# Where 48 VectorE dot products stand in a one-core transformer kernel: eight instead of twelve in each feed-forward loop, and eight in the output projection between them

## The chip, the cores and the metric

The kernel runs on one NeuronCore of one Trainium2 chip. The engines are named as in the profile: PE is TensorE (PEld its weight loads), DVE is VectorE, ACT is ScalarE, POOL is GpSimd and SP is SyncE. The metric is the device time of one execution in microseconds (us). Three executions of the kernel before took 1374.60, 1374.96 and 1375.77 us; the median is 1374.96 us.

## The reference

Three blocks in float32 are applied to x of 256 tokens by 1024 features: a sparse attention layer with a feed-forward, a retention layer with a feed-forward, and a state-space block whose norms are scaled and shifted by a modulation vector. Only the parts around the change are shown.

```python
def first_block(x, ...):
    for i in range(2):
        h = rms_norm(x, norm_mix_g[i])
        x = x + (dsa_mixer(h, ...) if i == 0 else retention_mixer(h, ...))
        x = x + conv_ffn(rms_norm(x, norm_ffn_g[i]), ...)
    return x

def conv_ffn(h, w_up, conv_w, conv_b, w_down):          # 1024 -> 2 * 2816 -> 1024
    u = h @ w_up
    u = sum(up[:, j:j + seq] * conv_w[j] for j in range(3)) + conv_b
    a, b = u[..., :2816], u[..., 2816:]
    return (jax.nn.silu(a) * b) @ w_down

def retention_mixer(h, w_in, out_g, w_out):
    ...                                                 # four heads
    return y.astype(h.dtype) @ w_out                    # 2048 -> 1024

def second_block(x, c, w_ada, b_ada, ...):
    mod = (jax.nn.silu(c) @ w_ada + b_ada)              # 6 * 1024 values
    shift_m, scale_m, gate_m, shift_f, scale_f, gate_f = jnp.split(mod, 6, axis=-1)
    h = rmsnorm(x, norm_mix_w) * (1.0 + scale_m) + shift_m
    ...
```

The change moves parts of the work on `silu(c) @ w_ada`. It needs nothing of x, and its result is first used after the second feed-forward.

## The kernel before

**Layout and split.** Activations are kept transposed, 128 features on the partitions by 256 tokens. Every float32 product is made of three matmuls: an operand is split into a high part (`w_hi`, `a_hi`, `b_hi`), which ACT makes by a copy, and a low part (`w_lo`, `a_lo`, `b_lo`), which DVE makes by a subtraction, and PE adds high by high, high by low and low by high (`mm3`, lines 182 to 184).

**The weight stream.** Weights come as 381 slabs of 128 by 1024 (512 KB) in the order of their use, through a ring of six buffers. SP loads slab s once DVE has split slab s - 6. `split_hi` on ACT (line 169) and `split_lo` on DVE (line 174) run three slabs ahead of PE. Each slab feeds 24 matmuls of 256 columns. At its end PE counts up `w_used`, for which those who read its result wait.

**The feed-forward** (`ffn_pe`, `ffn_act`, `ffn_vec`) goes over 22 pairs p of 128 columns of `a` and of `b`, three slabs a pair: two up slabs and one down slab. PE does the two up slabs of pair p + 1, and then the down slab of pair p, which needs `b_lo` of pair p (line 822). On DVE a pair is: split a slab, move the first half out of PSUM (`evict`, line 794), split a slab, two convolution taps (800, 802) on what ACT has scaled (741), move out the second half, two more taps, the product (818), split a slab, and `b_lo` (822). DVE and ACT run pairs 0 and 1 in straight code, pairs 2 to 17 in a loop of four turns with four pairs each (`UNROLL`, places u = 0 to 3), and pairs 18 to 21 again in straight code. After the last `b_lo`, `add_down` adds the result to `res` (853).

**The retention** (`retention_pe`, `_act`, `_vec`) is a loop of four turns, one a head with 12 slabs. Then comes the output projection (`out_pe`, `out_act`, `out_vec`) in straight code: eight output tiles m of two slabs. For each m DVE splits two slabs, waits until PE has done the tile, adds it to `res` (310) and makes `a_lo` of the tile before (275). ACT splits two slabs, waits for that add, and makes `a_hi` and the square `sq` of the new tile (266, 271). Both are queues in order, so a tile's slabs on ACT stand behind the add of the tile before on DVE. The second feed-forward's first slab needs `a_lo` and `sq` of all eight tiles, one after the other, and the sum of the squares (PE, 213) is what `vec_inv` (258 to 261) and `spread_inv` (228) turn into the norm's factor.

**The modulation** is 48 tiles of `w_ada` (128 by 1024, 512 KB each). Column i of `mod` is one tile multiplied by the row `silu(c)` and summed, in one DVE instruction (`dot`, line 336) with a short read of its accumulator behind it. POOL loads the tiles (`ada_loads`, line 331) into three buffers taken in turn: the load of tile i waits until dot i - 3 is done. The dots stand at three of the four places of each turn of both feed-forward loops (`LOOP_DOTS_AT = (0, 1, 3)`, 12 dots a loop) and at six places in each head (24 in all). In the loops a dot writes to `head_dots`, and at a turn's end one copy brings its columns to `mod` (837).

Of the kernel before, what the change touches and what calls it, by code (L numbers as in the profile page):

```python
# [21 lines left out]
HEADS_B = 4  # L22
# [13 lines left out]
S_BOUT = S_B + 12 * HEADS_B  # L36
# [10 lines left out]
ADA_TILES = 6 * NT  # L47
# [20 lines left out]
def val(base, it=None, step=0):  # L68

    return base if it is None else it * step + base  # L70
# [21 lines left out]
def build(nc, x, stream, ada, c_rows, params, consts, out):  # L92
    ctx = ExitStack()
    with ctx:
        def sb(name, shape, dt=F32):
            return ctx.enter_context(nc.sbuf_tensor(name, shape, dt))

        def sem(name):
            return ctx.enter_context(nc.semaphore(name))
# [17 lines left out]
        mod = sb("mod", [P, 48])  # L117
# [20 lines left out]
        def pcol(name, at=0, rows=P, n=1):  # L138
            return par[0:rows, COL[name] + at:COL[name] + at + n]
# [142 lines left out]
        def lo_ahead(dve, s, it=None, ds=0):  # L282
            if s < SLABS:
                split_lo(dve, s, it, ds)
# [17 lines left out]
                    hi_ahead(act, s + 3)  # L302
                act_prep(act, v, m, g)

        def out_vec(dve, s0, per, v, g):
            for m in range(NT):
                for s in range(s0 + per * m, s0 + per * (m + 1)):
                    lo_ahead(dve, s + 3)
                dve.wait_ge(w_used, s0 + per * (m + 1))
                dve.tensor_tensor(res[:, m], res[:, m], ps[:, 4 + (m + 2) % 4, 0:SEQ], ALU.add).then_inc(res_ready, 1)  # L310
                if m:
                    vec_prep(dve, v, m - 1, g)
            vec_prep(dve, v, NT - 1, g)


        FFN_DOTS, HEAD_DOTS = 12, 6
        assert 2 * FFN_DOTS + HEAD_DOTS * HEADS_B == ADA_TILES
        ada_base = ARENA - 4 * DM - 8
        top[0] = ada_base
        ada_raw, cond_row, head_dots = area(3, DM), area(DM), area(8)  # L320
        cond_in, cond_ready, mod_ready = sem("cond_in"), sem("cond_ready"), sem("mod_ready")
        ada_landed, dot_done = [sem(f"ada_landed{i}") for i in range(3)], sem("dot_done")

        def ada_loads(pool):

            pool.wait_ge(o_lo_ready, HEADS_A)
            pool.dma_start(cond_row, c_rows).then_inc(cond_in, 16)
            for i in range(ADA_TILES):
                if i >= 3:
                    pool.wait_ge(dot_done, i - 2)  # L330
                pool.dma_start(ada_raw[:, i % 3], ada[i]).then_inc(ada_landed[i % 3], 16)

        def dot(dve, i, o, it=None, per=0):

            dve.wait_ge(ada_landed[i % 3], val(16 * (i // 3 + 1), it, 16 * per // 3))
            dve.tensor_tensor_reduce(ada_raw[:, i % 3], ada_raw[:, i % 3], cond_row, 1.0, 0.0,  # L336
                                     ALU.mult, ALU.add, o).then_inc(dot_done, 1)


# [350 lines left out]

        UNROLL = 4
        LATER = (FF_PAIRS - 4) // UNROLL
        LOOP_DOTS_AT = (0, 1, 3)
        LOOP_DOTS = len(LOOP_DOTS_AT)
        assert LOOP_DOTS * LATER == FFN_DOTS
        assert (FF_PAIRS - 2) % UNROLL == 0
# [88 lines left out]
        def ffn_vec(dve, step, L, s0, v, next_gain):  # L785
            f = ffn_sems[L]

            def prm(p, j, it):
                c = COL[f"ffn{L}"] + 8 * p + j
                return par[:, c:c + 1] if it is None else par[:, bass.ds(it * 8 * UNROLL + c, 1)]  # L790

            def evict(p, half, s, it, ds):
                dve.wait_ge(w_used, val(s + half + 1, it, ds))
                dve.tensor_tensor(up[:, p % 2, half], ps[:, 6 - 2 * (p % 2) + half, 0:SEQ], inv[:, :], ALU.mult).then_inc(f["up_out"], 1)  # L794

            def taps(p, half, it):
                dve.wait_ge(f["tap"], val(2 * p + half + 1, it, 2 * UNROLL))
                t = conv[:, p % 2, half]
                u = up[:, p % 2, half]
                step(dve.scalar_tensor_tensor(out=t[:, 1:SEQ], in0=u[:, 0:SEQ - 1], scalar=prm(p, 3 * half + 1, it),  # L800
                                              in1=t[:, 1:SEQ], op0=ALU.mult, op1=ALU.add))
                dve.scalar_tensor_tensor(out=t[:, 2:SEQ], in0=u[:, 0:SEQ - 2], scalar=prm(p, 3 * half, it),  # L802
                                         in1=t[:, 2:SEQ], op0=ALU.mult, op1=ALU.add).then_inc(f["conv"], 1)

            def pair(p, s, it=None):
                ds = 0 if it is None else 3 * UNROLL
                lo_ahead(dve, s + 3, it, ds)
                if p == 0:
                    vec_inv(dve, step, v, EPS_A)
                    dve.wait_ge(inv_ready, v + 1)  # L810
                evict(p, 0, s, it, ds)
                lo_ahead(dve, s + 4, it, ds)
                taps(p, 0, it)
                evict(p, 1, s, it, ds)
                taps(p, 1, it)
                dve.wait_ge(f["conv"], val(2 * p + 2, it, 2 * UNROLL))
                dve.wait_ge(f["gate"], val(p + 1, it, UNROLL))
                dve.tensor_tensor(glu[:, p % 2], gate[:, p % 2], conv[:, p % 2, 1], ALU.mult).then_inc(f["glu"], 1)  # L818
                if p:
                    lo_ahead(dve, s + 5, it, ds)  # L820
                dve.wait_ge(f["hi"], val(p + 1, it, UNROLL))
                dve.tensor_tensor(b_lo[:, p % 2], glu[:, p % 2], b_hi[:, p % 2].bitcast(F32), ALU.subtract).then_inc(f["operand"], 1)  # L822

            pair(0, s0)
            pair(1, s0 + 2)
            dot0 = L * (FFN_DOTS + HEAD_DOTS * HEADS_B)
            if L == 0:
                dve.wait_ge(cond_ready, 1)
            with dve.Fori(0, LATER) as it:
                step.enter(it, 2 * UNROLL + 1)  # L830
                for u in range(UNROLL):
                    pair(2 + u, s0 + 5 + 3 * u, it)
                    if u in LOOP_DOTS_AT:
                        n = LOOP_DOTS_AT.index(u)
                        dot(dve, dot0 + n, head_dots[:, n:n + 1], it, LOOP_DOTS)
                dve.wait_ge(dot_done, val(dot0 + LOOP_DOTS, it, LOOP_DOTS))
                step(dve.tensor_copy(mod[:, bass.ds(it * LOOP_DOTS + dot0, LOOP_DOTS)], head_dots[:, 0:LOOP_DOTS]))
            step.leave(LATER)
            if L == 1:
                dve.tensor_tensor(mod[:, :], mod[:, :], pcol("b_ada", n=ADA_TILES), ALU.add).then_inc(mod_ready, 1)  # L840
            for p in range(2 + UNROLL * LATER, FF_PAIRS):
                pair(p, s0 + 3 * p - 1)
            lo_ahead(dve, s0 + 3 * FF_PAIRS - 1 + 3)
            add_down(dve, s0 + 3 * FF_PAIRS, v + 1, next_gain)
# [139 lines left out]
        def retention_vec(dve, step):  # L984
# [5 lines left out]
            with dve.Fori(0, HEADS_B) as it:  # L990
# [11 lines left out]
                for j in range(12):  # L1002
                    s = S_B + j
                    split_lo(dve, s + 3, it, HEAD)
                    if j in DOT_AT:
                        n = DOT_AT.index(j)
                        dot(dve, FFN_DOTS + n, head_dots[:, n:n + 1], it, HEAD_DOTS)
                    if j == 1:
                        rotary(q_rot, 0, s + 1)
                    if j == 3:  # L1010
                        dve.wait_ge(rot_ready, val(1, it, 2))
                        rotary(k_rot, 2, s + 1)
                    if j == 7:
                        dve.wait_ge(qk_ready, val(1, it, 1))
                        dve.tensor_tensor(decayed, ps[:, 7, 0:SEEN], con[:, bass.ds(it * SEEN + CC["decay"], SEEN)],
                                          ALU.mult).then_inc(decayed_ready, 1)
                    if j == 10:
                        dve.wait_ge(ret_sum, val(1, it, 1))
                        dve.tensor_scalar(rs_var[:, 0:NB], ps[:, 7, 400:402], 1.0 / 512, EPS_A, ALU.mult, ALU.add).then_inc(var_ready, 1)
                        rsqrt(dve, step, RS_RET, NB, rs_root[:, 0:NB], it)  # L1020
                        step(dve.tensor_scalar(diag[:, 2], ident, rs_root[:, 0:1], None, ALU.mult))
                        dve.tensor_scalar(diag[:, 3], ident, rs_root[:, 1:2], None, ALU.mult).then_inc(ret_diag, 1)
                    if j >= 8:
                        dve.wait_ge(w_used, val(s + 1, it, HEAD))
                        dve.tensor_tensor(g_b[:, j - 8], ps[:, j - 8, 0:SEQ], inv[:, :], ALU.mult).then_inc(g_taken, 1)
# [20 lines left out]
                y_lo(3)  # L1046
                dve.wait_ge(y_operand, val(4, it, 4))
            step.leave(HEADS_B)
            out_vec(dve, S_BOUT, 2, 3, "ffn_g1")


        top[0] = ARENA - 4 * SEQ
# [897 lines left out]
```

## Time and profile before

| | |
|---|---|
| median of the runs | 1374.96 us (1374.60 to 1375.77) |
| the profiled execution | 1374.81 us, of it 1372.8 us from the first to the last instruction |
| mean granted TensorE clock | 0.961 |
| PE, weight loads, DVE, ACT busy | 1277.5, 1238.6, 958.8, 706.3 us |
| first feed-forward's loop on DVE | 174 to 321 us, its pairs end at 351 us |
| retention heads, output projection | 367 to 540 us, 540 to 581 us |
| second feed-forward's loop on DVE | 607 to 753 us, its pairs end at 783 us |

Times in the rows are counted from the first instruction. In an answer in order of time each row is: start, duration, engine, line, operation, what it writes and reads, and in brackets how long the engine was idle before it and what ended that. Durations of instructions that follow each other overlap a little, so a step is read from start to start. A matmul's end is modelled; its start is not.

### The profile page before, as it was taken

To read this page: it belongs to the slowest core of one execution; us is meant where nothing else is said; L and a number is where in the kernel's file an instruction comes from. 1 tells how busy PE (TensorE), PEld (TensorE's weight loads), DVE (VectorE), ACT (ScalarE), POOL (GpSimd) and SP (SyncE) were. 2 spreads that over 40 slices of the span, in tenths; PEclk is the share of its full clock that TensorE was granted. 3 is DMA by queue.
4 is the path that set the end of the run, shared out by engine and by line. 5 is a ranking of instruction groups with operands and counts; after the bars stand their busy time and mean duration, and the time that the engine had idled before them with its cause. 6 is when DMAs were issued, how large, how long until landed. Compare 5 with 4: busy or idle time off the path is not lost.

```text
span 1372.8 us, 27337 instructions
## 1 busy us (share of the span) xinstructions
PE 1277.5 (93%) x9944; PEld 1238.6 (90%) x9944; DVE 958.8 (70%) x1728; ACT 706.3 (51%) x1098; POOL 28.8 (2%) x58
## 2 busy tenths in 40 slices
PE   6877999999899999999999989999999998999997
PEld 6867999999799899999999879898899997999996
DVE  4475688888678877568888868878777555555554
ACT  4334655555545455545555556666666334544442
POOL 0000000000000000000000000000000000000000
PEclk9889999999899999999999979999999998899998
DMA  6321456666366555636665506344345553455540
GB/s 257 123 62 63 175 206 212 218 220 208 108 245 245 189 207 215 211 128 214 229 214 168 199 33 229 132 160 156 135 138 170 183 184 123 139 184 183 183 153 31
DMA packets 70999, 234.54 MB, mean 171 GB/s; under 512 B 7056, under 2 KB 15376, under 8 KB 70304
## 3 DMA queue, kind: packets, MB, share of 16 engines
q1 hardware_dynamic: 63280, 203.87, 43.3%
q0 software_dynamic: 7664, 29.92, 6.3%
q8 instruction: 36, 0.59, 0.2%
q14 instruction: 19, 0.16, 0.0%
HBM read 232.69 MB, written 1.08 MB: 170 GB/s over the span
## 4 chain that ended last, share of the span: by engine, by line
PE 50%; DVE 29%; issue 10%; ACT 8%; DVEq 1%; DMA 0%; ACTq 0%; SPq 0%; PEldq 0%
PE ps L182 15%; PE ps L183 14%; PE ps L184 14%; DVE w_lo L174 11%; DVE arena L800 3%; ACT w_hi L169 3%; DVE arena L794 2%; DVE arena L802 2%; PE ps L213 2%; ACT arena L741 2%; DVE arena L1480 1%; DVE b_lo L822 1%; DVE arena L336 1%; ACT arena L544 1%; PE ps L1220 1%
## 5 line engine op out<-in xcount | busy, mean ns | idle before, releaser
L182 PE MATMUL ps<-a_hi,w_hi 128*128 128x256 f32 x1912 | 560.4, 293 | 11.1 <-DVE a_lo L1080 5.2
L174 DVE TENSOR_TENSOR w_lo<-w_raw,w_hi 128x1024 fp32r<-128x1024 f32 x381 | 462.2, 1220 | 148.6 <-ACT w_hi L169 144.7
L183 PE MATMUL ps<-a_lo,w_hi 128*128 128x256 f32 x1912 | 548.7, 287 | 0.0
L184 PE MATMUL ps<-a_hi,w_lo 128*128 128x256 f32 x1912 | 548.1, 287 | 0.0
L169 ACT ACTIVATE w_hi<-w_raw 128x1024 fp32r<-128x1024 f32 x381 | 387.0, 1046 | 18.8 <-PE ps L184 12.3
L182 PEld LDWEIGHTS ps<-a_hi,w_hi 128*128 128x128 f32 x1912 | 374.3, 196 | 23.2 <-issue 16.5
L183 PEld LDWEIGHTS ps<-a_lo,w_hi 128*128 128x128 f32 x1912 | 375.1, 196 | 0.5 <-issue 0.2
L184 PEld LDWEIGHTS ps<-a_hi,w_lo 128*128 128x128 f32 x1912 | 374.6, 196 | 0.0
L182 PE MATMUL ps<-b_hi,w_hi 128*128 128x256 f32 x928 | 267.1, 288 | 18.0 <-DVE b_lo L822 12.0
L183 PE MATMUL ps<-b_lo,w_hi 128*128 128x256 f32 x928 | 263.3, 284 | 0.0
L184 PE MATMUL ps<-b_hi,w_lo 128*128 128x256 f32 x928 | 263.2, 284 | 0.0
L182 PEld LDWEIGHTS ps<-b_hi,w_hi 128*128 128x128 f32 x928 | 178.5, 192 | 23.8 <-DVE w_lo L174 11.9
L183 PEld LDWEIGHTS ps<-b_lo,w_hi 128*128 128x128 f32 x928 | 178.8, 193 | 0.0
L184 PEld LDWEIGHTS ps<-b_hi,w_lo 128*128 128x128 f32 x928 | 178.7, 193 | 0.0
L741 ACT ACTIVATE arena<-arena,par 128x256 f32<-128x256 f32 x88 | 53.0, 602 | 107.9 <-DVE arena L794 107.9
L800 DVE SCALAR_TENSOR_TENSOR arena<-arena,par 128x255 f32<-128x255 f32 x88 | 42.3, 481 | 37.6 <-ACT arena L741 37.6
L336 DVE CUSTOM_DVE_ANT_0 arena<-arena 128x1024 f32<-128x1024 f32 x48 | 58.5, 1218 | 0.0
L752 ACT ACTIVATE b_hi<-arena 128x256 fp32r<-128x256 f32 x44 | 18.4, 419 | 63.1 <-DVE arena L818 63.1
L1637 ACT ACTIVATE arena<-ps 128x256 f32<-128x256 f32 x32 | 12.3, 384 | 73.6 <-PE ps L184 73.6
L802 DVE SCALAR_TENSOR_TENSOR arena<-arena,par 128x254 f32<-128x254 f32 x88 | 42.5, 483 | 10.2 <-DVE arena L800 2.0
L213 PEld LDWEIGHTS ps<-con,sq 128*128 128x128 f32 x224 | 36.3, 244 | 11.4 <-ACT sq L271 6.3
L213 PE MATMUL ps<-con,sq 128*128 128x1 f32 x224 | 35.6, 279 | 10.2 <-ACT sq L271 5.6
(245 smaller groups left out, 1208.4 us busy)
## 6 DMA issues: line engine op xcount, KB each, us to landing
w_raw<-stream SPq DMA_DIRECT2D x381, 512.0 KB, 3.7
arena<-ada POOLq DMA_DIRECT2D x48, 512.0 KB, 4.7
c_hi<-cum_rows POOLq DMA_DIRECT2D x4, 1024.0 KB, 5.0
con<-consts SPq DMA_DIRECT2D x1, 1440.0 KB, 13.0
arena<-x SPq DMA_DIRECT2D x1, 1024.0 KB, 5.1
out<-arena SPq DMA_DIRECT2D x2, 512.0 KB, 3.4
arena<-c_rows POOLq DMA_DIRECT2D x1, 512.0 KB, 7.7
par<-params SPq DMA_DIRECT2D x1, 319.0 KB, 5.5
```

The lines of the kernel that those rows point to most:

```text
L169: act.activation(w_hi[:, s % RING], w_raw[:, s % RING], ACT.Copy).then_inc(w_hi_ready, 1)
L174: dve.tensor_tensor(w_lo[:, s % RING], w_raw[:, s % RING], w_hi[:, s % RING].bitcast(F32), ALU.subtract).then_inc(w_lo_ready, 1)
L182: pe.matmul(o, wh, xh, start=start, stop=False, skip_group_check=shared)
L183: pe.matmul(o, wh, xl, start=False, stop=False, skip_group_check=shared)
L184: return pe.matmul(o, wl, xh, start=False, stop=stop, skip_group_check=shared)
L213: mm = pe.matmul(ps[:, sum_bank(v), b:b + 1], sq[:, k, b * P:(b + 1) * P], ones[:, 0:1], start=(k == 0 and b == 0), stop=(k == NT - 1), sk ...
L336: dve.tensor_tensor_reduce(ada_raw[:, i % 3], ada_raw[:, i % 3], cond_row, 1.0, 0.0, ALU.mult, ALU.add, o).then_inc(dot_done, 1)
L741: act.activation(conv[:, p % 2, half], up[:, p % 2, half], ACT.Identity, bias=prm(p, 6 + half, it), scale=prm(p, 3 * half + 2, it)).then_i ...
L752: act.activation(b_hi[:, p % 2], glu[:, p % 2], ACT.Copy).then_inc(f["hi"], 1)
L794: dve.tensor_tensor(up[:, p % 2, half], ps[:, 6 - 2 * (p % 2) + half, 0:SEQ], inv[:, :], ALU.mult).then_inc(f["up_out"], 1)
L800: step(dve.scalar_tensor_tensor(out=t[:, 1:SEQ], in0=u[:, 0:SEQ - 1], scalar=prm(p, 3 * half + 1, it), in1=t[:, 1:SEQ], op0=ALU.mult, op1= ...
L802: dve.scalar_tensor_tensor(out=t[:, 2:SEQ], in0=u[:, 0:SEQ - 2], scalar=prm(p, 3 * half, it), in1=t[:, 2:SEQ], op0=ALU.mult, op1=ALU.add). ...
```

## The change

The first loop and the second get two dots a turn instead of three (`LOOP_DOTS_AT = (0, 2)`, eight a loop), the heads keep six each, and the output projection gets eight, one for each tile m, between its slab splits and its wait for PE. These eight write straight to `mod`, with no copy. The buffer of a tile is now from a table: two buffers in turn in the feed-forward loops, three in turn in the heads and the projection. A load waits for the last dot on its buffer.

```diff
-        def out_vec(dve, s0, per, v, g):
+        def out_vec(dve, s0, per, v, g, first_dot):
             for m in range(NT):
                 for s in range(s0 + per * m, s0 + per * (m + 1)):
                     lo_ahead(dve, s + 3)
+                dot(dve, first_dot + m, mod[:, first_dot + m:first_dot + m + 1])
                 dve.wait_ge(w_used, s0 + per * (m + 1))
...
-        FFN_DOTS, HEAD_DOTS = 12, 6
-        assert 2 * FFN_DOTS + HEAD_DOTS * HEADS_B == ADA_TILES
+        FFN_DOTS, HEAD_DOTS, OUT_B_DOTS = 8, 6, 8
+        assert 2 * FFN_DOTS + HEAD_DOTS * HEADS_B + OUT_B_DOTS == ADA_TILES
+        DOT_BUF = [n % 2 for n in range(FFN_DOTS)] + [n % 3 for n in range(HEAD_DOTS * HEADS_B + OUT_B_DOTS)] + [n % 2 for n in range(FFN_DOTS)]
+        DOT_LOAD = [DOT_BUF[:i + 1].count(DOT_BUF[i]) for i in range(ADA_TILES)]
+        DOT_LAST = [max([j for j in range(i) if DOT_BUF[j] == DOT_BUF[i]], default=-1) for i in range(ADA_TILES)]
...
-                if i >= 3:
-                    pool.wait_ge(dot_done, i - 2)
-                pool.dma_start(ada_raw[:, i % 3], ada[i]).then_inc(ada_landed[i % 3], 16)
+                if DOT_LAST[i] >= 0:
+                    pool.wait_ge(dot_done, DOT_LAST[i] + 1)
+                pool.dma_start(ada_raw[:, DOT_BUF[i]], ada[i]).then_inc(ada_landed[DOT_BUF[i]], 16)
...
-        LOOP_DOTS_AT = (0, 1, 3)
+        LOOP_DOTS_AT = (0, 2)
...
-            out_vec(dve, S_BOUT, 2, 3, "ffn_g1")
+            out_vec(dve, S_BOUT, 2, 3, "ffn_g1", FFN_DOTS + HEAD_DOTS * HEADS_B)
```

DVE at the end of a turn of the feed-forward loop, before: `b_lo` of the last pair (822), the dot (336, two rows), the copy to `mod` and the next turn.

```order
L822 TENSOR_TENSOR b_lo<-arena,b_hi 128x256 [waits ffn0_hi]
L336 ISA arena<-arena 128x1024 [waits ada_landed2]
L336 ISA arena 128x1
L836 ISA
L837 ISA [waits dot_done]
L837 COPY mod<-arena 128x3
L82 REGISTER_ALU
```

The same place in the changed kernel:

```order
L826 TENSOR_TENSOR b_lo<-arena,b_hi 128x256 [waits ffn0_hi]
L840 ISA
L841 ISA [waits dot_done]
L841 COPY mod<-arena 128x2
L82 REGISTER_ALU
```

The turn's last pair has lost its dot; the one that stood in the second pair now stands in the third.

DVE at the start of the output projection, before: two splits (174), the add to `res` (310) that waits for PE, and from the second tile on `a_lo` (275).

```order
L990 COMPARE_AND_BRANCH
L174 TENSOR_TENSOR w_lo<-w_raw,w_hi 128x1024 [waits w_hi_ready] x2
L310 TENSOR_TENSOR res<-res,ps 128x256 [waits w_used]
L174 TENSOR_TENSOR w_lo<-w_raw,w_hi 128x1024 [waits w_hi_ready] x2
L310 TENSOR_TENSOR res<-res,ps 128x256 [waits w_used]
L275 SCALAR_TENSOR_TENSOR a_lo<-res,par,a_hi 128x256 [waits a_hi_ready]
```

The same place in the changed kernel, where the dot is line 340:

```order
L994 COMPARE_AND_BRANCH
L174 TENSOR_TENSOR w_lo<-w_raw,w_hi 128x1024 [waits w_hi_ready] x2
L340 ISA arena,mod<-arena 128x1024 [waits ada_landed0]
L340 ISA mod 128x1
L311 TENSOR_TENSOR res<-res,ps 128x256 [waits w_used]
L174 TENSOR_TENSOR w_lo<-w_raw,w_hi 128x1024 [waits w_hi_ready] x2
L340 ISA arena,mod<-arena 128x1024 [waits ada_landed1]
L340 ISA mod 128x1
L311 TENSOR_TENSOR res<-res,ps 128x256 [waits w_used]
L275 SCALAR_TENSOR_TENSOR a_lo<-res,par,a_hi 128x256 [waits a_hi_ready]
```

Each of the eight adds now stands behind a dot, and with it ACT's work on the tile.

## Rows read from the trace of the kernel before

**Rows 1.** The page, busy time of each engine and its share of the span.

```profile
PE 1277.5 (93%) x9944; PEld 1238.6 (90%) x9944; DVE 958.8 (70%) x1728; ACT 706.3 (51%) x1098; POOL 28.8 (2%) x58
```

**Rows 2.** Waits of PE in 175 to 351 and in 600 to 783: total, times, longest.

```profile
PE ps L182 <- DVE b_lo L822: 4.3, 11, 0.8
...
PE ps L182 <- DVE b_lo L822: 5.7, 10, 2.1
```

**Rows 3.** Waits of DVE, the longest in 315 to 352 and in 606 to 783.

```profile
DVE arena L800 <- ACT arena L741: 3.6, 5, 0.9
...
DVE arena L800 <- ACT arena L741: 17.4, 20, 0.9
```

**Rows 4.** Instructions in order of time, DVE, one turn of the first feed-forward's loop.

```profile
192.01 0.42 DVE L822 TENSOR_TENSOR b_lo<-arena,b_hi 128x256 fp32r<-128x256 f32 x1
192.35 1.22 DVE L336 CUSTOM_DVE_ANT_0 arena<-arena 128x1024 f32<-128x1024 f32 x1
...
193.49 1.22 DVE L174 TENSOR_TENSOR w_lo<-w_raw,w_hi 128x1024 fp32r<-128x1024 f32 x1
...
201.17 0.42 DVE L822 TENSOR_TENSOR b_lo<-arena,b_hi 128x256 fp32r<-128x256 f32 x1
...
209.23 0.42 DVE L822 TENSOR_TENSOR b_lo<-arena,b_hi 128x256 fp32r<-128x256 f32 x1
...
211.68 1.23 DVE L174 TENSOR_TENSOR w_lo<-w_raw,w_hi 128x1024 fp32r<-128x1024 f32 x1 [0.58 <-DVE mod L837]
...
219.45 0.42 DVE L822 TENSOR_TENSOR b_lo<-arena,b_hi 128x256 fp32r<-128x256 f32 x1
```

**Rows 5.** The same, PE: first matmuls of three down slabs in the last pairs.

```profile
337.43 0.28 PE L182 MATMUL ps<-b_hi,w_hi 128*128 128x256 f32 x1
...
346.07 0.28 PE L182 MATMUL ps<-b_hi,w_hi 128*128 128x256 f32 x1
...
351.15 0.39 PE L182 MATMUL ps<-b_hi,w_hi 128*128 128x256 f32 x1 [2.04 <-DVE b_lo L822]
```

**Rows 6.** The same, DVE: last pair of the first feed-forward.

```profile
347.07 0.42 DVE L794 TENSOR_TENSOR arena<-ps,inv 128x256 f32<-128x256 f32 x1
...
350.68 0.42 DVE L822 TENSOR_TENSOR b_lo<-arena,b_hi 128x256 fp32r<-128x256 f32 x1
```

**Rows 7.** The same, DVE: output projection, and start of the second feed-forward.

```profile
544.58 0.41 DVE L310 TENSOR_TENSOR res<-res,ps 128x256 f32<-128x256 f32 x1
546.83 2.36 DVE L174 TENSOR_TENSOR w_lo<-w_raw,w_hi 128x1024 fp32r<-128x1024 f32 x2 [1.83 <-ACT w_hi L169]
549.11 0.42 DVE L310 TENSOR_TENSOR res<-res,ps 128x256 f32<-128x256 f32 x1
...
581.41 0.42 DVE L310 TENSOR_TENSOR res<-res,ps 128x256 f32<-128x256 f32 x1 [1.15 <-PE ps L184]
...
582.41 0.48 DVE L275 SCALAR_TENSOR_TENSOR a_lo<-res,par,a_hi 128x256 fp32r<-128x256 f32 x1 [0.18 <-ACT a_hi L266]
583.66 1.23 DVE L174 TENSOR_TENSOR w_lo<-w_raw,w_hi 128x1024 fp32r<-128x1024 f32 x1 [0.77 <-ACT w_hi L169]
587.37 0.16 DVE L258 TENSOR_SCALAR rs_var<-ps 128x2 f32<-128x2 f32 x1 [2.49 <-PE ps L213]
...
588.91 0.29 DVE L261 TENSOR_SCALAR diag<-con,inv_tok 128x128 f32<-128x128 f32 x1
```

**Rows 8.** The same, PE: sum of the last tile's squares, and the norm's spread.

```profile
586.83 0.50 PE L213 MATMUL ps<-con,sq 128*128 128x1 f32 x4
...
590.51 0.59 PE L228 MATMUL ps<-diag,con 128*128 128x256 f32 x2
```

**Rows 9.** Stretches: busy time of PE, PEld, DVE, ACT, POOL; clock; DMA share, GB/s.

```profile
381.00:395.00 14.00, 14.00 (x77) 12.12 (x76) 10.26 (x16) 3.85 (x6) 1.59 (x3) 1.00 0.90 322
...
540.00:586.00 46.00, 45.84 (x384) 45.63 (x383) 26.85 (x34) 23.97 (x35) 0.00 (x0) 1.00 0.56 184
```

**Rows 10.** Line 331, all 48 loads of modulation tiles: issue to landing.

```profile
DMA to landing us min/median/max: 3.8/4.7/10.0
```

More of the change, by code:

```diff
@@ L328, in ada_loads, with dot @@
             for i in range(ADA_TILES):
-                if i >= 3:
-                    pool.wait_ge(dot_done, i - 2)
-                pool.dma_start(ada_raw[:, i % 3], ada[i]).then_inc(ada_landed[i % 3], 16)
-        def dot(dve, i, o, it=None, per=0):
-            dve.wait_ge(ada_landed[i % 3], val(16 * (i // 3 + 1), it, 16 * per // 3))
-            dve.tensor_tensor_reduce(ada_raw[:, i % 3], ada_raw[:, i % 3], cond_row, 1.0, 0.0,
+                if DOT_LAST[i] >= 0:
+                    pool.wait_ge(dot_done, DOT_LAST[i] + 1)
+                pool.dma_start(ada_raw[:, DOT_BUF[i]], ada[i]).then_inc(ada_landed[DOT_BUF[i]], 16)
+        def dot(dve, i, o, it=None, loads=0):
+            dve.wait_ge(ada_landed[DOT_BUF[i]], val(16 * DOT_LOAD[i], it, 16 * loads))
+            dve.tensor_tensor_reduce(ada_raw[:, DOT_BUF[i]], ada_raw[:, DOT_BUF[i]], cond_row, 1.0, 0.0,
                                      ALU.mult, ALU.add, o).then_inc(dot_done, 1)
@@ L825, in ffn_vec @@
             pair(1, s0 + 2)
-            dot0 = L * (FFN_DOTS + HEAD_DOTS * HEADS_B)
+            dot0 = L * (ADA_TILES - FFN_DOTS)
             if L == 0:
@@ L834, in ffn_vec @@
                         n = LOOP_DOTS_AT.index(u)
-                        dot(dve, dot0 + n, head_dots[:, n:n + 1], it, LOOP_DOTS)
+                        dot(dve, dot0 + n, head_dots[:, n:n + 1], it, LOOP_DOTS // 2)
                 dve.wait_ge(dot_done, val(dot0 + LOOP_DOTS, it, LOOP_DOTS))
@@ L1006, in retention_vec @@
                         n = DOT_AT.index(j)
-                        dot(dve, FFN_DOTS + n, head_dots[:, n:n + 1], it, HEAD_DOTS)
+                        dot(dve, FFN_DOTS + n, head_dots[:, n:n + 1], it, HEAD_DOTS // 3)
                     if j == 1:
```

## The prediction

> **What bounds the kernel now.** I first read the engines' shares [rows 1]: PE is busy for 93% of the span, DVE for 70%. By that alone, DVE instructions would cost nothing wherever they stand. So I read next who waits for whom in the feed-forwards, where the change takes dots away. PE waits there for `b_lo` of line 822, 11 times in the first and 10 times in the second [rows 2]. DVE waits for ACT and for itself, and its two lists hold no wait for PE, not even in the last pairs, where no dot stands [rows 3]. That is the point on which all rests: DVE is the slower engine for the whole of both feed-forwards. It enters the loop about level with PE, falls behind, and is still catching up when the last pair ends.
>
> The sizes come from one turn of the loop [rows 4]. From one `b_lo` to the next is 9.16 us where a dot stands between (192.01 to 201.17), 8.06 where none does (201.17 to 209.23), and 10.22 with the turn's last dot, the copy and the branch (209.23 to 219.45). Four pairs are 9.16 + 9.16 + 8.06 + 10.2 = 36.6 us. PE needs 8.64 us for a pair's 72 matmuls when nothing holds it (337.43 to 346.07) [rows 5], so 34.56 a turn: DVE is 2.0 us a turn behind. In the straight code after the loop its pair is about 7.5 us and it catches up, but in the last pair `evict` starts at 347.07 [rows 6], one microsecond after PE had the operand's slab done (346.07) [rows 5], and PE then stands 2.04 us before its last down slab, until `b_lo` of 350.68 is there. So the feed-forward ends with DVE's last `b_lo`, and everything behind it follows in a chain.
>
> The output projection is the opposite. From 564 us on DVE waits 1.15 us in each tile for PE (581.41 is the last) [rows 7], and weight loads are busy for 45.63 of 46 us [rows 9]. PE needs 2 x 2.88 = 5.76 us a tile (2.88 is a third of 8.64).
>
> **The change part by part.**
>
> *Four dots fewer in each feed-forward.* A dot takes DVE from 192.35 to 193.49, 1.14 us, with the accumulator's read inside it [rows 4]. Between pairs it shows as 9.16 - 8.06 = 1.10, because without it DVE waits 0.04 for ACT's split; at the turn's end there is no such wait. The new turn is 9.16 + 8.06 + 9.16 + (10.2 - 1.15) = 35.43 us, 1.15 less. Since DVE is never held by PE, the last `b_lo` comes 4 x 1.15 = 4.6 us earlier, and nothing else is late in its place until PE's own floor. That floor has to be worked out. A turn now keeps PE waiting for 35.43 - 34.56 = 0.87 us where it was 2.04. Before, PE lost 7.0 us on the way to its slab of 346.07; after, three turns and the first dot of the fourth make 3 x 0.87 + 0.5 = 3.1, so that slab starts 3.9 to 4.0 earlier, at 342.1. The last pair's `evict` comes 4.6 earlier, at 342.5. DVE is still the later of the two by 0.3 us, so the 4.6 is got in full, and there is hardly any more to be got. The second feed-forward is the same code; it starts 1.1 us better (ACT does the `silu` of c only in the first), the same steps give the same margin, and again 4.6. Sum: 9.2 us.
>
> Bounds for the turn's end, which the trace does not show without a dot: the copy waits for the dot's semaphore, and about 0.2 us a turn may go with it; but the register work for the copy and the branch, which ran under the dot, may now come out by as much. So 1.15 +- 0.2 a turn, 3.8 to 5.4 a loop. I take the middle, since the two are alike in size.
>
> *Eight dots in the output projection.* By count there is room: 1.15 us of waiting a tile, and a dot is 1.14. But the tile is a round through two queues, and the first tiles have to be read, where DVE is behind and nothing waits for PE. From one add to the next are 4.53 us (544.58 to 549.11) [rows 7]: add, ACT's `a_hi` and `sq`, ACT's first split, DVE's two splits. The dot stands in this round, not beside it, so the round becomes 4.53 + 1.15 = 5.68 us, 0.08 less than PE's 5.76. DVE starts the projection late, and now never catches up: the first add comes at 544.58 + 1.15 = 545.73, the eighth at 545.73 + 7 x 5.68 = 585.49, where it was 581.41 [rows 7]. That is 4.1 us later. PE is not held inside the projection: the split for its sixth slab ends at 549.2 (545.73 + 2.25 + 1.2), and PE, whose last slab ends at 581.2, comes to that slab at 549.5; from there the room grows by 0.08 a tile.
>
> What does the late last add hold? `a_lo` of the last tile begins 1.0 after the add and takes 0.48, so it is there at 587.0; PE took that tile at 586.83 [rows 8], because it had to do seven others first. So PE loses 0.2 to 0.3 us here, not 4.1. DVE's next split moves with ACT from 583.66 to 587.7 and ends at 588.9, so `vec_inv` starts at 588.9 instead of 587.37, 1.5 later, and its last step ends at 588.91 + 0.29 + 1.5 = 590.7 [rows 7]. PE comes to the spread at 590.51 + 0.3 [rows 8]. They meet within 0.1. Everything from there to the first down slab is one chain, so I charge 0.35 us. Ends: 0, if DVE's operations overlap better; 2.5, if the round is 5.9 instead of 5.68, when the last add comes 1.5 later still, `vec_inv` with it, and PE stands 0.3 longer.
>
> *Two buffers in the feed-forwards.* A load waits for the dot two before and has more than 17 us (two pairs) to land, and the 48 loads took 3.8 to 10.0 [rows 10]. In the projection a tile is asked for three rounds ahead, 15 us. Both cost nothing. The added traffic is 8 x 0.52 MB in 46 us, 91 GB/s on top of 184 [rows 9]. That is 275, and 322 was moved in the stretch from 381 us [rows 9].
>
> *The heads* keep their dots and their places. Nothing is charged.
>
> Sum against the profiled execution: 1374.81 - 9.2 + 0.35 = 1365.96. That execution lies 0.15 below the median, so I say **1366.0 us**.
>
> **The rivals.**
>
> *1. The turn's end gives a little more.* 0.2 us a turn saved at the copy gives 2 x 5.3 = 10.6, which is also PE's floor, since the evict would then start as PE ends. With a projection that costs nothing this is 1374.81 - 10.6 = 1364.2, and runs of one kernel spread over 1.2 us, so 1363.0 to 1364.6. For it: the wait for the dot's semaphore is real. Against it: the register rows stay.
>
> *2. Only part comes through.* If PE, not DVE, sets the last pairs, only the shorter waits for `b_lo` are won, 3.9 a loop: 1374.81 - 7.8 + 0.35 = 1367.4. Together with the projection's upper end, 2.5, it is 1369.5. For it: the margin between them is 0.3 us.
>
> *3. The round in the projection becomes longer than PE's tile.* The point is 5.76 us, and I put it at 5.68. At 6.3 PE is paced by it: 8 x 0.54 = 4.3 us, and the late opening of the second feed-forward costs some 3 more. 1366 + 7 = 1373, no change that a measurement can tell. For it: only 0.08 us of room. Against it: every part of the round has a row, and a dot adds 1.14 wherever one stands.
>
> *4. Slower than before: the tiles of `w_ada` are not there in the projection.* A dot stands at the head of DVE's queue there, and behind it the add, ACT's splits, and then PE. The round can't be shorter than a third of (landing + 1.15 + 0.5). To lose the 9.2 and 3 us more, it must be 5.76 + 12.2 / 8 = 7.3, a landing of 20 us: 1366 + 12.2 = 1378. It decides from 16 us on. Against it: the longest landing was 10.0 [rows 10], and 322 GB/s have been moved [rows 9].
>
> The Trainium skill has a rule that speaks for this rival: the page SBUF — State Buffer (section "SBUF: two separate sides"), says that a DMA issued from POOL has its descriptors written by POOL's own cores, which a two-port operation of DVE locks out, so that the transfer waits for DVE. By it, landings would grow with DVE's busy share, which the dots raise in the projection. No landing in this trace bears it out.
>
> **How the numbers follow.** The forecast (1364.6 to 1367) has 0.58, rival 1 0.12, rival 2 0.17, rival 3 0.08 and rival 4 0.04; 0.01 is for others. From 1363.0 to 1370.0 the range takes in the forecast, rivals 1 and 2, and the unknown ends (3.8 a loop with 0.35 gives 1367.6, with 2.5 1369.7). Rivals 3 and 4 lie outside. A measurement of this kernel can tell about 0.2%, 2.75 us, from no change, so faster is below 1372.2: faster 0.87, same 0.08, slower 0.05.
>
> **What would show it.** In the profile after: `b_lo` to `b_lo` at 9.16, 8.06, 9.16 and 9.05 in a turn; the last `b_lo` of the first feed-forward at 346.1 us, and no wait of DVE for PE before it, or a very short one; PE's wait before the last down slab 0.6 shorter. In the projection adds 5.68 apart, the last one 4.1 later against PE's last slab, with no wait of DVE for PE in the later tiles and none of PE; the spread 0.3 to 0.4 later. DVE's busy sum unchanged. I am wrong if PE waits for `w_lo` inside the projection (rival 3), if a dot there is idle before it (rival 4), or if DVE waits for PE for long in pairs 18 to 21 (rival 2).

## The result, and the profile after

The changed kernel takes **1361.95 us** (median of four runs, 1361.85 to 1362.55). The kernel before, on the same chip, takes 1375.37 (four runs, 1374.60 to 1375.91). The ratio is 0.9904, with a 95% interval from 0.9887 to 0.9921: 13.4 us faster. 1366.0 was predicted, with a range from 1363.0 to 1370.0. The direction was right and the gain about half as large again as forecast, so the time lies 1 us below the range.

The page, for [rows 1]: the same 48 dots, the same work, a shorter span.

```profile
span 1359.8 us, 27345 instructions
...
PE 1274.5 (94%) x9944; PEld 1238.1 (91%) x9944; DVE 957.6 (70%) x1728; ACT 706.3 (52%) x1098; POOL 28.8 (2%) x58
```

Waits of PE in the two feed-forwards (170 to 347 and 596 to 779), for [rows 2]: total, times, longest.

```profile
PE ps L182 <- DVE b_lo L826: 1.5, 2, 1.2
...
PE ps L182 <- DVE b_lo L826: 1.8, 3, 1.3
```

Eleven and ten waits have become two and three, and the longest, before the last down slab, has gone from 2.0 and 2.1 us to 1.2 and 1.3.

DVE in order of time, the end of a turn and the pair after it, for [rows 4]; then the last pair, for [rows 6], with PE's matmul that waits for it, for [rows 5].

```profile
200.95 0.42 DVE L826 TENSOR_TENSOR b_lo<-arena,b_hi 128x256 fp32r<-128x256 f32 x1
...
210.12 0.41 DVE L826 TENSOR_TENSOR b_lo<-arena,b_hi 128x256 fp32r<-128x256 f32 x1
210.45 0.16 DVE L841 COPY mod<-arena 128x2 f32 x1
211.19 1.23 DVE L174 TENSOR_TENSOR w_lo<-w_raw,w_hi 128x1024 fp32r<-128x1024 f32 x1 [0.58 <-DVE mod L841]
...
218.95 0.42 DVE L826 TENSOR_TENSOR b_lo<-arena,b_hi 128x256 fp32r<-128x256 f32 x1
...
228.10 0.42 DVE L826 TENSOR_TENSOR b_lo<-arena,b_hi 128x256 fp32r<-128x256 f32 x1
```

```profile
342.52 0.42 DVE L798 TENSOR_TENSOR arena<-ps,inv 128x256 f32<-128x256 f32 x1
...
346.13 0.42 DVE L826 TENSOR_TENSOR b_lo<-arena,b_hi 128x256 fp32r<-128x256 f32 x1
```

```profile
346.60 0.39 PE L182 MATMUL ps<-b_hi,w_hi 128*128 128x256 f32 x1 [1.24 <-DVE b_lo L826]
```

The steps are 9.17, 8.83 and 9.15 us here. The middle one, over the turn's end, is the one to look at: the next split starts 1.07 us after `b_lo`, where it was 2.45 (209.23 to 211.68) [rows 4]. The copy starts 0.33 after `b_lo`, where it started 1.70 after it; before, it came 0.22 behind the start of the dot's short accumulator read:

```profile
210.71 0.08 DVE L336 DVE_READ_ACCUMULATOR2_ANT arena<- 128x1 f32 x1
210.93 0.17 DVE L837 COPY mod<-arena 128x3 f32 x1
```

Behind the copy DVE idles 0.58 us in both traces.

DVE in the output projection and behind it, for [rows 7], and PE there, for [rows 8].

```profile
541.30 0.41 DVE L311 TENSOR_TENSOR res<-res,ps 128x256 f32<-128x256 f32 x1
543.54 2.36 DVE L174 TENSOR_TENSOR w_lo<-w_raw,w_hi 128x1024 fp32r<-128x1024 f32 x2 [1.83 <-ACT w_hi L169]
545.82 1.22 DVE L340 CUSTOM_DVE_ANT_0 arena<-arena 128x1024 f32<-128x1024 f32 x1
...
546.97 0.41 DVE L311 TENSOR_TENSOR res<-res,ps 128x256 f32<-128x256 f32 x1
...
580.97 0.41 DVE L311 TENSOR_TENSOR res<-res,ps 128x256 f32<-128x256 f32 x1
...
583.22 1.23 DVE L174 TENSOR_TENSOR w_lo<-w_raw,w_hi 128x1024 fp32r<-128x1024 f32 x1 [0.77 <-ACT w_hi L169]
584.36 0.15 DVE L258 TENSOR_SCALAR rs_var<-ps 128x2 f32<-128x2 f32 x1
```

```profile
582.74 0.50 PE L213 MATMUL ps<-con,sq 128*128 128x1 f32 x4
...
586.42 0.59 PE L228 MATMUL ps<-diag,con 128*128 128x256 f32 x2
```

The round is 5.67 us (541.30 to 546.97), and no add waits for PE any more.

**Where the 13.0 us of span went.** PE runs the same 9944 matmuls in both traces, so each of them can be compared by its start. The differences of the stretches between the same two matmuls, in us:

| stretch (us in the trace before) | before | after | difference |
|---|---|---|---|
| first transpose to the loop of the first feed-forward (6 to 167) | 160.64 | 160.81 | +0.17 |
| first feed-forward to its last down slab (167 to 351) | 184.07 | 178.59 | -5.48 |
| its end and the opening of the first head (351 to 373) | 22.29 | 22.44 | +0.15 |
| heads, projection, opening of the second feed-forward (373 to 596) | 222.77 | 223.08 | +0.31 |
| second feed-forward to its last down slab (596 to 783) | 186.66 | 181.16 | -5.50 |
| from there to the last transposes (783 to 1367) | 584.48 | 581.88 | -2.60 |

The rest is 0.0 (x came 0.8 us later, and behind PE's last instruction there is 0.8 less). So 11.0 us came where the loops lost dots, 0.3 were paid in the projection, and 2.3 us, all told, came from stretches in which no instruction has been touched. The last row is that, less the 0.32 by which the first and the third are longer. In it PE has runs of matmuls that start 0.213 us apart instead of 0.120, and they stand elsewhere in the two traces. Compared step by step, 42 matmuls of the last row take the long step only before, worth 3.92 us, and 13 only after, worth 1.27: 2.65 net, which is the whole row. Busy time and granted clock of PE in two such places, before (783 is the last down slab of the second feed-forward) and the same matmuls after:

```profile
782.80:786.40 3.60, 3.52 (x17) 0.53 0.65 212
1042.60:1046.00 3.40, 3.40 (x19) 0.52 0.78 270
```

```profile
773.20:776.80 3.60, 3.13 (x24) 1.00 0.63 205
1031.30:1034.70 3.40, 3.40 (x31) 1.00 0.85 282
```

Before, PE stood at the lower level (0.5 of the full clock, 1.2 GHz) for both; after, at the full one. Each is worth some 15 matmuls of 0.213 - 0.120 = 0.093 us, 1.4 us.

### The profile page after: what moved, and what is told of

Same layout as the page of the kernel before. It is cut to its first block, busy times and chain, and to the rows that moved or that the text cites. A ratio compares the mean times of both kernels' runs of the same rounds, so it can differ in the third digit from the quotient of the medians.

```text
span 1359.8 us, 27345 instructions
## 1 busy us (share of the span) xinstructions
PE 1274.5 (94%) x9944; PEld 1238.1 (91%) x9944; DVE 957.6 (70%) x1728; ACT 706.3 (52%) x1098; POOL 28.8 (2%) x58
## 4 chain that ended last, share of the span: by engine, by line
PE 51%; DVE 29%; issue 9%; ACT 9%; DVEq 1%; DMA 1%; ACTq 0%; SPq 0%; PEldq 0%
PE ps L182 15%; PE ps L184 14%; PE ps L183 14%; DVE w_lo L174 12%; ACT w_hi L169 3%; DVE arena L804 3%; DVE arena L798 2%; PE ps L213 2%; DVE arena L806 2%; ACT arena L745 2%; DVE arena L1484 1%; DVE b_lo L826 1%; DVE arena L340 1%; ACT arena L548 1%; PE ps L1224 1%
## 5 line engine op out<-in xcount | busy, mean ns | idle before, releaser
L806 DVE SCALAR_TENSOR_TENSOR arena<-arena,par 128x254 f32<-128x254 f32 x88 | 42.5, 483 | 10.2 <-DVE arena L804 2.0
```

## The experiments

The account after the result was: DVE's own sequence paces the loops, and a turn gained 1.4 us by its lost dot, not 1.15, because the dot had stood at the turn's end; the projection costs 0.3; the rest is half-rate stretches that moved. Its rivals were that the projection's dots give something, and that the whole 13 us is work.

**The projection's dots left out.** The loads of their tiles are left out too, so eight columns of `mod` stay zero and the kernel is not the whole computation.

```diff
                 for s in range(s0 + per * m, s0 + per * (m + 1)):
                     lo_ahead(dve, s + 3)
-                dot(dve, first_dot + m, mod[:, first_dot + m:first_dot + m + 1])
                 dve.wait_ge(w_used, s0 + per * (m + 1))
```

> The changed kernel with the eight dots of the output projection and the loads of their tiles left out (their eight columns of the modulation vector are set to zero at the start, so that part of the computation is missing). It gives the loops' gain alone, and against the changed kernel the price of the eight dots. My account: the stretch between the two norms' spreads around the projection costs 0.35 to 0.5 us less, so 1361.5 us; the opening of the second feed-forward stands as in the kernel before. Rival: the eight dots are free or even help, and the time is 1361.9 or more. Rival: the loops gain only what I had forecast, and something in the projection gave the rest of the gain; then this kernel is near 1366.

Measured: 1362.06 us (1359.83 to 1362.70), ratio 0.9899 (0.9883 to 0.9916). The time alone can't tell it from the changed kernel. The starts can: from a matmul in the opening of the first head (373.44 before) to the sums of the last tile's squares behind the projection PE takes 213.42 us, as in the kernel before, where the changed kernel takes 213.73. The eight dots cost 0.31 us. The loops' stretches are 178.65 and 181.41, so their gain is there without the projection's part.

**The projection's dot ahead of the splits.**

```diff
+                dot(dve, first_dot + m, mod[:, first_dot + m:first_dot + m + 1])
                 for s in range(s0 + per * m, s0 + per * (m + 1)):
                     lo_ahead(dve, s + 3)
-                dot(dve, first_dot + m, mod[:, first_dot + m:first_dot + m + 1])
```

> The changed kernel with each dot of the output projection ahead of the tile's two splits, where DVE waits 1.4 to 1.9 us for ACT, instead of behind them. If the round add, ACT, splits, dot is what made the last add late, the round goes back to 4.5 us, the last add is at PE's end again, and 0.4 to 0.5 us come back: 1361.5. If DVE's busy time in the projection is what counts, nothing changes: 1361.95.

Measured: 1359.64 us (1358.52 to 1360.84), ratio 0.9885 (0.9868 to 0.9901). Its 213.43 us in that stretch are again those of the kernel before. DVE there, in order of time:

```profile
543.82 0.41 DVE L311 TENSOR_TENSOR res<-res,ps 128x256 f32<-128x256 f32 x1
544.15 0.48 DVE L275 SCALAR_TENSOR_TENSOR a_lo<-res,par,a_hi 128x256 fp32r<-128x256 f32 x1
544.55 1.22 DVE L340 CUSTOM_DVE_ANT_0 arena<-arena 128x1024 f32<-128x1024 f32 x1
...
546.06 2.36 DVE L174 TENSOR_TENSOR w_lo<-w_raw,w_hi 128x1024 fp32r<-128x1024 f32 x2 [0.29 <-ACT w_hi L169]
548.34 0.42 DVE L311 TENSOR_TENSOR res<-res,ps 128x256 f32<-128x256 f32 x1
...
576.13 0.42 DVE L311 TENSOR_TENSOR res<-res,ps 128x256 f32<-128x256 f32 x1 [1.15 <-PE ps L184]
```

The dot runs in DVE's wait for ACT, of which 0.29 us is left, the round is 4.52 us, and the last add waits for PE again. So it was the dot's place in the round, not DVE's load, that made the adds late. Of the 2.3 us by which the median beats the changed kernel's, 0.3 is this; the rest is not explained by any instruction.

**Three dots a turn, none at its end.**

```diff
-        LOOP_DOTS_AT = (0, 1, 3)
+        LOOP_DOTS_AT = (0, 1, 2)
```

> The kernel before with its three dots a turn at places 0, 1, 2 instead of 0, 1, 3: as many dots, none at the turn's end. If a dot at the turn's end costs more than one inside (the copy to the modulation vector waits for the dot's semaphore), a turn becomes 0.2 to 0.3 us shorter and the eight turns 1.7 to 2.2, so 1373.3 us. If the register work that ran under the dot comes out instead, nothing changes or it is slower: 1375.3 to 1377. A stretch at the lower TensorE clock may come or go with the shift, 1.5 us either way; it is told apart by the matmuls' starts.

Measured: 1370.64 us (six runs, 1363.98 to 1371.31), ratio 0.9958 (0.9940 to 0.9977). DVE at a turn's end:

```profile
247.34 0.42 DVE L822 TENSOR_TENSOR b_lo<-arena,b_hi 128x256 fp32r<-128x256 f32 x1
247.68 0.16 DVE L837 COPY mod<-arena 128x3 f32 x1
248.38 1.23 DVE L174 TENSOR_TENSOR w_lo<-w_raw,w_hi 128x1024 fp32r<-128x1024 f32 x1 [0.55 <-DVE mod L837]
...
256.15 0.42 DVE L822 TENSOR_TENSOR b_lo<-arena,b_hi 128x256 fp32r<-128x256 f32 x1
```

From one `b_lo` to the next over the turn's end are 8.81 us, and a dot inside brings a pair to 9.16. A turn is 36.3 us instead of 36.6. From the second `b_lo` to the last, DVE takes 175.85 us (176.96 before) and 174.82 (175.97 before): 1.1 and 1.15 less with as many dots. So a dot at the turn's end costs 1.4 us, and inside 1.1. The time is 4.7 us lower than before, though, not 2.3. The six runs spread over 7.3 us, and the traced one, 1367.50, is 3.1 below their median. Behind the second feed-forward's last down slab its trace takes 5.4 us less than the kernel before, and 5.3 of them are the long steps (64 matmuls only before, 10 only here). No trace shows what the median is made of.

**Two dots a turn, one at its end.**

```diff
-        LOOP_DOTS_AT = (0, 2)
+        LOOP_DOTS_AT = (1, 3)
```

> The changed kernel with its two dots a turn at places 1 and 3 instead of 0 and 2: as many dots, one of them at the turn's end. With dots at 0, 1, 2 a turn was 0.30 us shorter than at 0, 1, 3. So here a turn is 0.30 us longer than in the changed kernel, 35.5 against 35.2, and a loop takes 1.1 to 1.2 us more from its second b_lo to its last. Two loops: 1364.2, give or take the half-rate stretches. If the 1.4 us that a turn gained per removed dot had another cause than the turn's end, the stretches are as in the changed kernel.

Measured: 1367.01 us (1365.70 to 1367.18), ratio 0.9933 (0.9914 to 0.9951). Second `b_lo` to the last: 173.42 and 171.99 us, against 171.53 and 170.47 in the changed kernel. That is 1.9 and 1.5 more, where 1.1 to 1.2 was expected. The turn's end is 10.2 again, and the pair after it, here without a dot, is 8.2 instead of 8.07; 0.08 of this 0.14 lies before a split and 0.05 before the first tap, both of which need ACT's result; why ACT is later there was not found. In the first loop's first turn that pair takes 8.46. The two loops' 3.4 us are most of the 4.1 by which it is slower, when each is counted against the kernel before that was measured beside it (1376.37 and 1375.37).

**The loop dots in the wait for ACT**, in the kernel before:

```diff
                 evict(p, 1, s, it, ds)
+                if between:
+                    between()
                 taps(p, 1, it)
...
-                    pair(2 + u, s0 + 5 + 3 * u, it)
-                    if u in LOOP_DOTS_AT:
-                        n = LOOP_DOTS_AT.index(u)
-                        dot(dve, dot0 + n, head_dots[:, n:n + 1], it, LOOP_DOTS)
+                    def between(u=u):
+                        if u in LOOP_DOTS_AT:
+                            n = LOOP_DOTS_AT.index(u)
+                            dot(dve, dot0 + n, head_dots[:, n:n + 1], it, LOOP_DOTS)
+                    pair(2 + u, s0 + 5 + 3 * u, it, between)
```

> The kernel before (12 dots a loop, at 0, 1, 3) with each loop dot moved from behind the pair's last instruction to behind its second evict, where DVE waits 0.92 us for ACT's scaling. If DVE's own sequence of instructions and waits paces the feed-forwards, a dot costs 1.15 - 0.92 = 0.23 us there, a pair 8.3 us, less than PE's 8.64, so PE sets the pace: nearly all of its 13 us of waits for b_lo go, and some 0.9 us at each loop's last down slab: 1359 to 1361. Rival: ACT, which then has its silu and the high part of the product later, takes DVE's place, and a pair with a dot stays near 9.16: 1370 or more.

Measured: 1361.46 us (1359.04 to 1362.85), ratio 0.9901 (0.9884 to 0.9917), with all 24 loop dots in place and none in the projection. DVE in order of time in a pair with a dot, and then its waits in 200 to 345:

```profile
237.75 0.42 DVE L794 TENSOR_TENSOR arena<-ps,inv 128x256 f32<-128x256 f32 x1
238.09 1.22 DVE L336 CUSTOM_DVE_ANT_0 arena<-arena 128x1024 f32<-128x1024 f32 x1
...
239.24 0.48 DVE L800 SCALAR_TENSOR_TENSOR arena<-arena,par 128x255 f32<-128x255 f32 x1
```

```profile
DVE arena L800 <- ACT arena L741: 5.4, 7, 0.9
DVE arena L794 <- PE ps L184: 4.1, 10, 0.5
```

The tap starts right behind the dot, 1.49 us after the evict; without a dot it was 1.34 (229.49 to 230.83 in the same trace). The dot costs 0.15 us instead of 1.1. And now DVE's list holds what was nowhere in [rows 3], a wait for PE: PE sets the pace for part of the loop, and PE's own list for 170 to 346 has one wait left, 1.2 us before the last down slab. The loops' stretches are 177.72 and 181.29 us. With twelve dots a loop they are about as short as with the changed kernel's eight (178.59 and 181.16).

**Both moved**: the changed kernel with its loop dots behind the evict and its projection dots ahead of the splits.

> The changed kernel with its loop dots behind the pair's second evict and its projection dots ahead of the splits. The kernel with only the loop dots moved had PE at its own pace in both loops, so here the loops can't be faster than there (177.7 and 181.3 us from the first down slab of a loop to the last), and the projection costs 0.3 less than in the changed kernel. Structure says 1.0 to 1.3 us less than the changed kernel with its dots after the pair, in the loops, and 0.3 in the projection: 1360.3, give or take the half-rate stretches. If DVE's waits in the loops mattered further, it would be 1358 or less.

Measured: **1359.15 us** (1358.54 to 1360.12), ratio 0.9882 (0.9865 to 0.9898), the best of the kernels here beside the one with only the projection's dots moved (1359.64, which it overlaps): 16.7 and 15.7 us below the kernels before that were measured beside them. The loops are at 177.72 and 181.31 us, the first head to the sums at 213.42. The first loop and the projection gained 0.9 and 0.3 on the changed kernel, the second nothing (181.16 there, with no half-rate stretch at its opening, which this one has: 16 matmuls, 1.5 us). From 175 to 347 us PE is busy for 170.76 of 172, so in the first loop there is hardly more to gain on DVE.

**The half-rate stretches.** A memset on DVE in the chain that opens the retention delays all that follows, and changes no work. It was put into the kernel before and into the changed one, in three sizes:

```diff
             dve.wait_ge(inv_ready, 3)
+            step(dve.memset(arena[:, 512:512 + 820], 0.0))
             dve.tensor_tensor(cos_i, const("cos", SEQ), inv[:, :], ALU.mult).then_inc(g_taken, 1)
```

> The kernel before with one memset of 820 elements a partition on DVE in the chain that opens the retention, about 0.85 us on the path that everything behind it follows. It adds no work to PE and only moves what follows. If the matmuls at half rate stand where the work of the stage puts them, the time is 1375.3 + 0.9 = 1376.2, and the list of half-rate stretches is that of the kernel before. If their places and lengths hang on when a stage begins, the list changes from 560 us on, and the time with the delay taken off lies up to 3 us away, more likely below, since the changed kernel and the one with dots at 0, 1, 2 both lost stretches that the kernel before has.

> The same with 1640 elements, about 1.7 us. Without any hanging on the start: 1377.0. With it: 1372 to 1377, with another list of half-rate stretches than at 0.85.

> The same with 2460 elements, about 2.6 us. Without: 1377.9. With it: 1373 to 1378, with a list of its own.

> The changed kernel with the memset of 820 elements at the opening of the retention (about 0.8 us on the path). The kernel before came out 1.1 to 2.5 us lower than its own time once three such delays were taken off, so its own place was a slow one. If the changed kernel's is a common or a lucky one, its time with the delay taken off is its own or higher: 1361.95 + 0.8 = 1362.8, up to 1365. If the change is worth 13 us whatever the place, it too comes out about 2 lower: 1360.7.

> The same with 1640 elements (about 1.5 us): 1363.4 to 1365 by the first account, 1361.5 by the second.

> The same with 2460 elements (about 2.3 us): 1364.2 to 1366 by the first account, 1362.3 by the second. The mean of the changed kernel over the four places against the mean of the kernel before over its four is what the change is worth without the half-rate stretches: by the rows of DVE and PE 10.6 us.

The memsets put 0.78, 1.46 and 2.14 us on the path (from the memset's start to the next instruction, as in these two rows of the first).

```profile
367.83 0.74 DVE L987 MEMSET arena<- 128x820 f32 x1 [1.93 <-ACT inv L253]
368.61 0.42 DVE L988 TENSOR_TENSOR arena<-con,inv 128x256 f32<-128x256 f32 x1
```

| delay, us | before, us (runs) | less the delay | changed, us (runs) | less the delay |
|---|---|---|---|---|
| none | 1375.81 (25) | 1375.8 | 1361.95 (4) | 1361.95 |
| 0.78 | 1374.42 (8) | 1373.6 | 1364.77 (2) | 1364.0 |
| 1.46 | 1374.76 (8) | 1373.3 | 1365.39 (2) | 1363.9 |
| 2.14 | 1376.86 (8) | 1374.7 | 1363.44 (2) | 1361.3 |
| mean | | 1374.4 | | 1362.8 |

A kernel that is 0.8 us longer on its path ran 1.4 us faster. With the delay taken off, the same work lies between 1373.3 and 1375.8 before, and between 1361.3 and 1364.0 after. Stretches appear and vanish with the delay. In the kernel before with 0.78 us, PE is at the lower level in the second feed-forward's opening, where it was at the full one. Its last down slab, from 786.30 here, begins at the full level and falls to the lower one after 12 matmuls, where it was at the lower one from the start for 15:

```profile
603.80:607.00 3.20, 3.20 (x17) 0.51 0.52 166
...
785.70:787.30 1.60, 1.00 (x8) 1.00 0.27 38
787.30:789.50 2.20, 2.20 (x15) 0.63 0.75 246
```

The delay is not all that moves them. In the trace with 1.46 us PE is at the lower level right behind the first feed-forward's last down slab, where the kernel before is at the full one, and up to there, ahead of the memset, the two run the same instructions:

```profile
351.10:354.50 3.40, 3.14 (x24) 1.00 0.70 189
...
351.30:354.70 3.40, 3.36 (x16) 0.52 0.63 192
```

So one trace of a place does not say which stretches belong to it; the medians of eight and more runs say that the kernel before stands at an unlucky one of its four places, 1.4 us above their mean. That the changed kernel stands at a lucky one is not shown. Its delays have two runs each, and they stand beside a kernel before of 1376.37 us, where 1361.95 stands beside 1375.37. Counted from the kernel before beside them, the four places of the changed kernel (less the delay) lie 13.4, 12.4, 12.4 and 15.1 us lower. The means of the table are 11.6 us apart, and 11.9 when counted in this way. Each is known to about 1 us: the kernel before had medians of 1375.4, 1375.8 and 1376.4 us beside the different sets of kernels here. The rows of DVE and PE account for 5.48 + 5.50 - 0.31 = 10.7.

## Why the prediction was wrong, and where it was right

*The bound: right.* DVE paced both feed-forwards to their ends. Moving the dots into DVE's wait for ACT, with their number in the loops unchanged, brought DVE's first waits for PE and took 6.4 and 5.4 us off the two stretches.

*Four dots fewer a loop, 4.6 us: the mis-sized term.* It measured 5.48 and 5.50. The step that failed is the turn's end. "I take the middle, since the two are alike in size", I wrote of the wait for the dot's semaphore, and of register work that might come out in its place. They are not alike. The wait for the semaphore was the 0.22 us between the accumulator's read and the copy, and it went. The register work gave nothing back: the idle time behind the copy is 0.58 us with the dot and without it. So the next split comes 1.38 sooner, not 1.15, and the step over the turn's end is 8.83 us where 9.05 was forecast. The three dots at 0, 1, 2 show the same 0.3 us a turn with nothing else changed. Four turns of 35.2 instead of 35.4 us make 0.9 a loop, 1.8 us in all. That is rival 1, which I gave 0.12; its 10.6 us for both loops were close to the 11.0 measured.

Two marks of the forecast agree by chance. It put the last `evict` at 342.5 and the last `b_lo` at 346.1, and they started at 342.52 and 346.13. But PE's first matmul came 0.77 us later in this trace (7.21, where it was 6.44), and this hid most of the 0.9 that the loop had gained beyond the forecast. Counted from the first matmul, both came some 0.7 earlier than forecast. PE's floor was just touched: the last `evict` starts 0.2 us after PE's down slab at 342.32, where it was 1.0 (347.07 and 346.07), and the step to the last `b_lo` is 7.58 us instead of 7.51.

*The projection, 0.35 us: right, and by its own steps.* Round 5.67 (5.68 predicted), last add 4 us late against PE, no wait for PE in any tile, price 0.31. Rival 3's point of 5.76 was not reached. Rival 4's place was the projection, and there no dot waited for its tile; one did, for 0.64 us, in a retention head. The landings were 4.1 to 9.4 us for all 48 (4.6 to 5.3 in the projection), where the longest was 10.0 before [rows 10]. So the rule that spoke for rival 4 in the Trainium skill, SBUF — State Buffer (section "SBUF: two separate sides"), did not show here. It speaks of two-port operations of DVE, and nothing here tells whether the dots or the splits are such; the forecast's "landings would grow with DVE's busy share" went further than the rule.

*The clock: a term put at nothing.* About 2.7 us of the 13.4 is none of this; in the two traces it is 2.3. The sum had no term for stretches at half rate, and gave no reason. The range got 1.2 us for the spread of the runs, from three of them; 25 runs of the kernel before on one chip spread over 2.8 us (1374.57 to 1377.37), and moving everything behind the retention's opening by 1.5 us changed its median, less the delay, by 2.5. With the turn's end at its right size the sum would have said 1374.81 - 11.0 + 0.3 = 1364.1, inside the range. From there to 1361.95 are 2.2 us, and between the two traces the half-rate steps of the last row account for 2.65. So of the 4.0 us by which the forecast was off, 1.8 are the turn's end and 2.2 the missing term, and it is the second that put the time outside the range. That the gain is 13.4 and not near 11 is in part luck: the kernel before stands 1.4 us above the mean of its four places.

What stays open: which of the half-rate stretches come with which place, and why they differ between traces ahead of any change, was not found out. That they make up the 2.2 us is read from one trace of each kernel; no experiment holds them fixed. Why ACT costs a pair without a dot 0.14 us behind a turn's end was not found either.

## What to carry to other kernels

An engine at 70% of the span can be the one that paces a stage: look in its list of waits for the engine that seems to be the bound, and if that is missing, an instruction taken off it shortens the stage, until the other engine's pace is reached (a wait of DVE for PE appeared here once the dots cost 0.15 us). Before such work is moved elsewhere, look for a wait inside the same sequence: a 1.15 us dot product behind the evict cost 0.15, and ahead of the splits nothing, where behind them it stood in a round between two queues. And compare kernels that differ by 1% at more than one place in time and beside each other: the same work moved by 1.5 us ran 2.5 us faster here, less the delay, and the kernel before alone had medians from 1375.3 to 1376.4 us beside the different sets.

## What the runs showed of the hardware

A half-rate stretch cost nothing where PE was not the bound. In the changed kernel PE is at the lower level at the first feed-forward's opening:

```profile
167.80:171.00 3.20, 3.20 (x17) 0.51 0.34 91
```

PE does 15 matmuls there in 1.4 us more, but the steps of `b_lo` go on unchanged (8.08, 9.13, 9.16). The kernel before with 0.78 us of delay shows it alone: it has 15 half-rate matmuls in the opening of the second feed-forward, where the kernel before has none (the row from 603.80 above), and from there to the last down slab it takes 186.72 us, against 186.66. PE's waits for `b_lo` from 600 to 675 us are 0.3 us instead of 1.2. Where PE was the bound they cost their full price: behind the second feed-forward's last down slab 0.093 us each, 2.65 us net between the two kernels, out of 2.60.
